# Depthwise convolution of the conv module: six channel tiles on TensorE and two on VectorE in place of five and three

## The chip, the cores and the metric

The kernel runs on one core of one Trainium2 chip. The time is the device time of one execution in microseconds (us). A profile of one execution records every instruction of the five engines: TensorE (PE, with its weight loads as PEld), VectorE (DVE), ScalarE (ACT), GpSimd (POOL) and SyncE (SP), which here only issues DMAs.

## The reference

The program computes one inference step of a two-layer decoder, for 512 prompt tokens and 8 x 8 sample tokens (576 columns in all), model width 1024, in float32. The first layer has a Conformer convolution module between two feed-forward blocks, the second has dilated attention between two more. The part that matters here is that module:

```
def conformer_conv(h, prev, w_pw1, b_pw1, w_dw, b_dw, ln_g, ln_b, w_pw2, b_pw2):
    a, g = jnp.split(h @ w_pw1 + b_pw1, 2, axis=-1)
    u = a * jax.nn.sigmoid(g)
    u_ext = jnp.concatenate([prev.astype(u.dtype), u], axis=1)
    c = lax.conv_general_dilated(u_ext, w_dw[:, None, :].astype(u.dtype), window_strides=(1,),
                                 padding='VALID', dimension_numbers=('NWC', 'WIO', 'NWC'),
                                 feature_group_count=CONV_INNER) + b_dw
    c = jax.nn.silu(layernorm(c, ln_g, ln_b))
    return c @ w_pw2 + b_pw2, u_ext[:, -(CONV_WIDTH - 1):]
```

The depthwise convolution gives every one of the 1024 channels its own 31 taps over time. The LayerNorm behind it needs the mean over all channels, so it can't begin before the last channel tile is convolved.

## The kernel before

Activations lie with channels on the 128 partitions, in KD = 8 channel tiles, and tokens along the free axis. The order of the work is written out by hand for each engine; engines wait for one another through semaphores, and each engine and each DMA queue works its list in order.

**The stage.** The pointwise projection pw1 is 16 chunks c of 128 output channels, two for each channel tile ct (the value half and the gate half). For each chunk ACT and then DVE split the float32 weights into a high and a low part (L995, L1488), PE runs 48 matmuls (L2101), DVE scales the result out of PSUM (L1844), and after the second chunk of a tile ACT applies the sigmoid (L1261) and DVE writes `u` for that tile into `ucat` (L1855, L1856) and raises `u_ready`. The weight buffers and PSUM banks let PE be some two chunks ahead of DVE: chunk c waits for its own split and for the scaled-out result of chunk c-2.

**Two ways to convolve.** The constant CD is how many of the eight tiles go to DVE, and CP = KD - CD is how many go to PE.
- On DVE (function `taps`), a tile is 31 taps, each a pair of instructions, one over the 512 prompt columns (L1828) and one over the 64 sample columns (L1829). In the tiles behind the first one ACT does the first tap (L1255, L1257). DVE does a few taps whenever the list has room: 4 after each even chunk, and `taps(3 if ct <= CD else 12)` after each tile, for tiles 1 to 6; what is left follows behind the chunk loop.
- On PE (function `convolve`), a tile is 32 matmuls of 512 columns and 32 of 64 columns (L2401, L2407), each with 32 output channels and the taps as its weights `dW`. These weights are made by POOL (L901). The input `uV` is four shifted copies of the tile's `ucat`, made by DMAs, eight of them on SP's queue (function `spread`, L677) and eight on POOL's (L936), into one of two buffers. ACT brings the result from PSUM to `cT` (`conv_out`, L1243, L1244).

**Places.** The first tile for PE is tile CD. Its convolve stands behind chunk 2*CD + 4, the following ones behind each odd chunk from 2*CD + 5 on, and the last behind the chunk loop. Behind each convolve but the first of the loop stands `mean_of` (L2421), which adds one finished tile into the sum for the LayerNorm's mean; the others stand behind the loop. On SP the uV loads of tile ct stand behind the weight load of chunk 2*ct + 7. On ACT `conv_out(ct - 1 - CD)` stands behind the sigmoid of tile ct.

**The end of the stage.** PE: the last chunk, a convolve, a `mean_of`, transposes of the new state (L2456, L2458), more `mean_of`, the last convolve, bias tables (L2467, L2468), `mean_of(7)`, one more bias table (L2473, which waits for ACT's cast of the table E2, L1289), and `mean_of(CD - 1)`. Then DVE subtracts the mean (L1867), ACT squares (L1302), PE sums (L2496) and pw2 follows. ACT casts E2 only behind the last `conv_out`. SP loads the tables E, after waiting for `uv_in0` to show three uV loads, behind its last `spread`.

Of the kernel before, what the change touches and what calls it, by code (L numbers as in the profile page):

```python
# [18 lines left out]
HALF = TOK // 2  # L19
KD, KF = D // P, FF // P  # L20
CW = 31
CD = 3
CP = KD - CD
NQ, NS = 4, 8
HEADS, HD, AW = 8, 64, 512
# [262 lines left out]
def trunk_program(nc, I, O):  # L288
# [286 lines left out]
    def _(sp):  # L575
# [91 lines left out]
        def spread(ct):  # L667

            n = ct - CD
            sp.wait_ge(S["u_ready"], ct + 1)  # L670
# [15 lines left out]

        done = CD
        for c in range(4, 24):
# [170 lines left out]
    def _(pool):  # L859
# [37 lines left out]
        def taps(n):  # L897

            if n >= 2:
                pool.wait_ge(S["conv_mm"], n - 1)  # L900
            nc.gpsimd.tensor_tensor(  # L901
                dW[:, n % 2], id32[:].rearrange("p (a b c) -> p a b c", a=1, b=1).broadcast_to([P, 4, NS, 32]),
                wQ[:, :, CD + n, :].rearrange("p a (b c) -> p a b c", c=1).broadcast_to([P, 4, NS, 32]),
                ALU.mult).then_inc(S["taps_ready"], 1)
# [23 lines left out]
        for n in range(CP):  # L928
            taps(n)

            pool.wait_ge(S["u_ready"], CD + n + 1)
            if n == 0:
                pool.wait_ge(S["st_ready"], KD)
            for g in range(2, 4):
                for q in range(NQ):
                    pool.dma_start(uV[32 * q:32 * q + 32, n % 2, g, :],  # L936
                                   ucat[32 * g:32 * g + 32, CD + n, q:q + VW]).then_inc(S[f"uv_gp{n % 2}"], 16)

# [1905 lines left out]
```

## Time and profile before

| what | us |
|---|---|
| median of 3 runs | 2265.07 |
| lowest and highest run | 2263.11, 2266.39 |
| time of the profiled execution | 2262.11 |
| its span, first to last instruction | 2260.2 |
| pw1 chunks 3 to 15 with the convolutions, on PE | 440.85 to 571.9 |
| LayerNorm and its surroundings, until pw2's first matmul on PE | 571.9 to 592.3 |

Starts in the rows below are counted from the span's start. A row of PE stands for a run of matmuls of one line; those of the convolution and of the mean, in plain float32, count as two each, those of pw1 as one. PEclk is the clock that TensorE was granted, 1.00 being its upper level of 2.4 GHz and 0.50 its lower of 1.2 GHz.

### The profile page before, as it was taken

What the parts mean: (1) busy time and instruction counts of PE and PEld (TensorE: products, weight loads), DVE (VectorE), ACT (ScalarE), POOL (GpSimd) and SP (SyncE); (2) the same over time, 40 slices, a digit from 0 to 9 for tenths busy, and PEclk for the clock granted to TensorE, in tenths of its full rate; (3) what the DMA queues carried; (4) which work ended last, traced back from release to release, by engine and by line L of the source; (5) the groups of instructions that cost most, each with busy time, mean ns of one, the idle gap of its engine ahead of it and who ended that gap; (6) DMA issues with size and microseconds to landing.
All of it is one profiled execution on the core that took longest, in us unless ns stands there. A gap on an engine that the chain in (4) does not pass through costs nothing.

```text
span 2260.2 us, 41620 instructions
## 1 busy us (share of the span) xinstructions
PE 2214.9 (98%) x17636; PEld 2102.0 (93%) x17636; DVE 1617.6 (72%) x2138; ACT 890.1 (39%) x1167; POOL 137.3 (6%) x191
## 2 busy tenths in 40 slices
PE   7999999999999999999999999999999999999998
PEld 6999999987799999998889999999987789999998
DVE  7983995699789849953358956984445479947963
ACT  6431443222654314432234422442145555413442
POOL 0000000323010000001001000001001100000001
PEclk8999999999899999999999999999999999999999
DMA  5543443554244435423439533532959933233321
GB/s 156 158 151 110 151 156 93 164 141 126 72 147 150 140 100 164 153 83 90 132 107 304 173 114 99 168 115 73 240 148 281 253 113 94 75 98 96 88 77 55
DMA packets 372091, 305.61 MB, mean 135 GB/s; under 512 B 13798, under 2 KB 338414, under 8 KB 371050
## 3 DMA queue, kind: packets, MB, share of 16 engines
q1 hardware_dynamic: 365485, 232.06, 36.4%
q0 software_dynamic: 6464, 71.76, 9.2%
q8 instruction: 86, 1.41, 0.3%
q14 instruction: 44, 0.35, 0.1%
q10 hardware_dynamic: 12, 0.02, 0.0%
HBM read 284.45 MB, written 70.54 MB: 157 GB/s over the span
## 4 chain that ended last, share of the span: by engine, by line
PE 88%; DVE 6%; issue 2%; ACT 2%; DMA 2%; SPq 1%; DVEq 0%; ACTq 0%
PE ps L2101 34%; PE ps L2157 13%; PE ps L2159 13%; PE ps L2158 13%; PE ps L2565 2%; PE ps L2563 2%; PE ps L2564 2%; PE ps L2401 2%; PE ps L2609 1%; DMA kc<-in_cache_kv_w 1%; DVE blk L1572 1%; PE ps L2725 1%; DVE hlS L1549 1%; PE ps L2663 1%; PE ps L2716 1%
## 5 line engine op out<-in xcount | busy, mean ns | idle before, releaser
L1087 ACT CAST hlS<-blk 128x1024 fp32r<-128x1024 f32 x176 | 184.3, 1053 | 207.0 <-PE ps L2159 169.4
L2101 PE MATMUL ps<-actH,oWA 128*128 128x288 f32 x1408 | 250.4, 296 | 0.0
L2101 PE MATMUL ps<-actH,oWB 128*128 128x288 f32 x1408 | 250.0, 296 | 0.0
L1716 DVE SCALAR_TENSOR_TENSOR cs<-ps,rstd 128x576 f32<-128x576 f32 x64 | 48.5, 757 | 246.9 <-PE ps L2101 246.9
L1549 DVE TENSOR_TENSOR hlS<-blk,hlS 128x1024 fp32r<-128x1024 f32 x176 | 213.5, 1216 | 2.4 <-ACT hlS L1087 2.4
L2157 PE MATMUL ps<-tM,hlA 128*128 128x288 f32 x704 | 212.4, 302 | 2.9 <-DVE hlA L1549 2.4
L2157 PE MATMUL ps<-tE,hlS 128*128 128x288 f32 x704 | 208.5, 296 | 4.1 <-DVE hlS L1549 4.1
L2101 PEld LDWEIGHTS ps<-actH,oWA 128*128 128x128 f32 x1408 | 209.0, 189 | 1.2 <-DVE cs L1611 0.6
L2101 PEld LDWEIGHTS ps<-actH,oWB 128*128 128x128 f32 x1408 | 209.0, 189 | 0.0
L2157 PE MATMUL ps<-tM,hlS 128*128 128x288 f32 x704 | 208.2, 296 | 0.0
L2158 PE MATMUL ps<-tM,hlA 128*128 128x288 f32 x704 | 208.0, 295 | 0.0
L2159 PE MATMUL ps<-tM,hlA 128*128 128x288 f32 x704 | 207.5, 295 | 0.0
L2158 PE MATMUL ps<-tE,hlS 128*128 128x288 f32 x704 | 207.5, 295 | 0.0
L2159 PE MATMUL ps<-tE,hlS 128*128 128x288 f32 x704 | 207.2, 294 | 0.0
L2158 PE MATMUL ps<-tM,hlS 128*128 128x288 f32 x704 | 207.2, 294 | 0.0
L2159 PE MATMUL ps<-tM,hlS 128*128 128x288 f32 x704 | 206.9, 294 | 0.0
L1488 DVE TENSOR_TENSOR wHL<-wst,wHL 128x1024 fp32r<-128x1024 f32 x64 | 82.2, 1285 | 116.8 <-ACT wHL L995 116.7
L1116 ACT ACTIVATE ta<-ta 128x576 f32<-128x576 f32 x88 | 60.5, 687 | 266.5 <-DVE ta L1631 266.5
L2101 PE MATMUL ps<-hH,wHL 128*128 128x288 f32 x896 | 158.5, 297 | 0.0
L1549 DVE TENSOR_TENSOR hlA<-blk,hlA 128x1536 fp32r<-128x1536 f32 (+2 forms) x104 | 156.0, 1504 | 0.9 <-ACT hlA L1087 0.9
L1087 ACT CAST hlA<-blk 128x1536 fp32r<-128x1536 f32 (+2 forms) x104 | 132.3, 1280 | 47.6 <-PE ps L2101 29.7
L2101 PE MATMUL ps<-actL,oWA 128*128 128x288 f32 x704 | 150.8, 296 | 0.0
(323 smaller groups left out, 5363.3 us busy)
## 6 DMA issues: line engine op xcount, KB each, us to landing
blk<-in_ffn_w_in SPq DMA_DIRECT2D x352, 256.0 KB, 4.1
raws<-in_ffn_w_out SPq DMA_DIRECT2D x64, 704.0 KB, 4.7
out_kv_sample<-in_cache_kv_w POOLq DMA_DIRECT2D x8, 4064.0 KB, 16.8
out_kv_sample<-in_cache_kv_w POOLq DMA_DIRECT2D x8, 2016.0 KB, 9.2
wst<-in_conv_w_pw SPq DMA_DIRECT2D x24, 512.0 KB, 4.1
wst<-in_w_kv SPq DMA_DIRECT2D x24, 512.0 KB, 3.8
kc<-in_cache_kv_w SPq DMA_DIRECT2D x40, 256.0 KB, 9.1
kc<-in_cache_kv_w SPq DMA_DIRECT2D x8, 1024.0 KB, 7.7
```

The costliest lines, as they stand in the source:

```text
L1087: nc.scalar.copy(o, a).then_inc(S["f_h"], 1)
L1116: nc.scalar.activation(ta[:], ta[:], ACT.Silu).then_inc(S["silu_done"], 1)
L1488: nc.vector.tensor_tensor(wL[:, s % 2, 0:size], wst[:, s, 0:size], wH[:, s % 2, 0:size].bitcast(f32), ALU.subtract).then_inc(S["w_ready"], 1)
L1549: nc.vector.tensor_tensor(o, a, h.bitcast(f32), ALU.subtract).then_inc(S["f_ready"], 1)
L1716: nc.vector.scalar_tensor_tensor(px[m % 2], pair(2 + m % 2), 0.5, rstd[:], ALU.mult, ALU.mult).then_inc(S["px_ready"], 1)
L2101: nx = nc.tensor.matmul(outs[t], a, b[:, t, :], start=start and first, stop=stop and b is xh and not first)
L2157: nc.tensor.matmul(out, wh[:, cols], TERM[what][:, p, 0], start=p == 0, stop=False)
L2158: nc.tensor.matmul(out, wh[:, cols], TERM[what][:, p, 1], start=False, stop=False)
L2159: nx = nc.tensor.matmul(out, wl[:, cols], TERM[what][:, p, 0], start=False, stop=p == KD // 2 - 1)
L2401: nc.tensor.matmul(ps[32 * g:32 * g + 32, 0, :], dW[:, s, g, k, :], uV[:, s, g, 4 * k:4 * k + SEQ], start=k == 0, stop=k == NS - 1, tile_p ...
L2563: nc.tensor.matmul(ps[:, t, :], xh, a, start=k == 0, stop=False)
L2564: nc.tensor.matmul(ps[:, t, :], xh, b, start=False, stop=False)
```

## The change

One constant is changed. Everything in the stage that depends on it moves with it.

```
@@ -19,7 +19,7 @@
 HALF = TOK // 2
 KD, KF = D // P, FF // P
 CW = 31
-CD = 3
+CD = 2
 CP = KD - CD
 NQ, NS = 4, 8
 HEADS, HD, AW = 8, 64, 512
```

Tile 2 goes from DVE to PE, so there are six convolves. On PE the first of them stood behind chunk 10, with nothing of the kind ahead of it, and one followed behind chunk 11:

```order
L2101 MATMUL ps<-hH,wHL 128x288 x2
L2401 MATMUL ps<-uV,dW 32x512 x32
L2407 MATMUL ps<-uV,dW 32x64 x32
L2101 MATMUL ps<-hH,wHL 128x288 x2
L2101 MATMUL ps<-hL,wHL 128x288 x2
```

Now there is one behind chunk 8 and, after another chunk, this one behind chunk 9, with a `mean_of`; those behind chunks 11, 13, 15 and behind the loop stand where they did:

```order
L2101 MATMUL ps<-hH,wHL 128x288 x2
L2401 MATMUL ps<-uV,dW 32x512 x32
L2407 MATMUL ps<-uV,dW 32x64 x32
L2421 MATMUL ps<-cT,ones 128x288 x2
L2101 MATMUL ps<-hH,wHL 128x288 x2
L2101 MATMUL ps<-hL,wHL 128x288 x2
```

What moved is one convolve, with its `mean_of`, into the chunk loop: the one behind chunk 10 is gone, and those behind chunks 8 and 9 are new. Behind the loop PE's list loses one `mean_of`, ahead of the last convolve:

```order
 L2456 MATMUL ps<-ident,ucat 30x128 x8
 L2458 MATMUL ps<-ident,un 64x128 x8
-L2421 MATMUL ps<-cT,ones 128x288 x6
+L2421 MATMUL ps<-cT,ones 128x288 x4
 L2401 MATMUL ps<-uV,dW 32x512 x32
 L2407 MATMUL ps<-uV,dW 32x64 x32
```

On DVE the 30 pairs of taps of tile 2 are gone, and since `taps(3 if ct <= CD else 12)` gives 12 from tile 3 on, nine taps of the remaining tiles come earlier: behind the `u` of tile 3, ahead of the weight split of chunk 10. At the end of the loop DVE's list now reads, from the last split of pw1 to the LayerNorm, with no tap in it:

```order
L1488 TENSOR_TENSOR wHL<-wst,wHL 128x1024
L1844 TENSOR_TENSOR tb<-ps,rstd 128x576
L1855 SCALAR_TENSOR_TENSOR ucat<-ta,par,tb 128x512
L1856 SCALAR_TENSOR_TENSOR ucat<-ta,par,tb 128x8x8
L1844 TENSOR_TENSOR ta<-ps,rstd 128x576
L1844 TENSOR_TENSOR tb<-ps,rstd 128x576
L1855 SCALAR_TENSOR_TENSOR ucat<-ta,par,tb 128x512
L1856 SCALAR_TENSOR_TENSOR ucat<-ta,par,tb 128x8x8
L1488 TENSOR_TENSOR wHL<-wst,wHL 128x1024
L1867 SCALAR_TENSOR_TENSOR cT<-ps,cT 128x576 x8
```

What moved there is the work that stood between these rows: 24 pairs of taps came after the last L1856 before, and none does now.

On SP and POOL there is one more uV load of eight DMAs each, and POOL makes the weights of one more tile. SP's row of uV loads for the first PE tile stands one pair of weight loads earlier (behind chunk 11's load, not chunk 13's). On ACT the first tap of tile 2 goes, and `conv_out` of the first PE tile comes in, both in the list of tile 3. The waits for `uv_in0` are counted as before (three loads), and the load of the sixth PE tile goes to the other buffer, so SP's loads of the tables E no longer wait for the last uV load to land.

## Rows read from the trace of the kernel before

**Rows 1.** The page's first part: each engine's busy time in the span.

```profile
PE 2214.9 (98%) x17636; PEld 2102.0 (93%) x17636; DVE 1617.6 (72%) x2138; ACT 890.1 (39%) x1167; POOL 137.3 (6%) x191
```

**Rows 2.** The chain that ended last, in time order: start us, us, what.

```profile
440.85 51.20 PE ps L2101 x384
...
514.42 1.17 PE ps L2421 x4
...
550.22 7.00 PE ps L2401 x64
...
561.03 2.91 PE ps L2421 x12
563.94 7.00 PE ps L2401 x64
570.95 0.94 PE ps L2407 x64
```

**Rows 3.** Busy time by stretch: us, engines (instructions), PEclk, DMA share, GB/s.

```profile
485.00:575.00 90.00, 89.60 (x984) 61.28 (x983) 84.11 (x155) 20.89 (x29) 26.12 (x44) 1.00 0.50 137
575.00:600.00 25.00, 22.22 (x146) 16.41 (x147) 19.64 (x29) 21.00 (x31) 0.00 (x0) 0.73 0.15 43
```

**Rows 4.** DVE in time order near the LayerNorm: start, us, instruction, [idle before].

```profile
574.42 0.75 DVE L1828 SCALAR_TENSOR_TENSOR cT<-ucat,par,cT 128x512 f32<-128x512 f32 x1
...
575.40 0.75 DVE L1828 SCALAR_TENSOR_TENSOR cT<-ucat,par,cT 128x512 f32<-128x512 f32 x1
576.07 0.28 DVE L1829 SCALAR_TENSOR_TENSOR cT<-ucat,par,cT 128x64 f32<-128x64 f32 x1
...
577.71 5.41 DVE L1867 SCALAR_TENSOR_TENSOR cT<-ps,cT 128x576 f32<-128x576 f32 x8 [0.23 <-PE ps L2421]
```

**Rows 5.** PE in time order, the same stretch.

```profile
574.89 1.19 PE L2473 MATMUL ps<-E2r,sel 128*128 128x512 f32 x4 [0.40 <-ACT E2r L1289]
...
576.44 1.24 PE L2421 MATMUL ps<-cT,ones 128*128 128x288 f32 x4
```

**Rows 6.** ACT in time order, the same stretch.

```profile
572.49 0.31 ACT L1244 ACTIVATE cT<-ps,par 128x64 f32<-128x64 f32 x1
572.69 2.15 ACT L1289 CAST E2r<-E 128x2352 fp32r<-128x2352 f32 x1
...
578.75 0.67 ACT L1302 ACTIVATE ta<-cT 128x576 f32<-128x576 f32 x1
```

**Rows 7.** Everything on tile cT, the taps' line: duration ns min/median/max, first and last start.

```profile
L1828 DVE SCALAR_TENSOR_TENSOR cT<-ucat,par,cT x90: 740/752/2456, 445.2 to 575.4; 128x512 f32<-128x512 f32 x90
```

**Rows 8.** DVE in time order inside the pointwise stage: ends of tiles 2, 3 and 7.

```profile
465.33 0.28 DVE L1856 SCALAR_TENSOR_TENSOR ucat<-ta,par,tb 128x64 f32<-128x64 f32 x1
...
477.45 0.28 DVE L1856 SCALAR_TENSOR_TENSOR ucat<-ta,par,tb 128x64 f32<-128x64 f32 x1
...
480.48 1.22 DVE L1488 TENSOR_TENSOR wHL<-wst,wHL 128x1024 fp32r<-128x1024 f32 x1
...
552.59 0.28 DVE L1856 SCALAR_TENSOR_TENSOR ucat<-ta,par,tb 128x64 f32<-128x64 f32 x1
```

**Rows 9.** SyncE's queue in time order: start, us that the issuing took.

```profile
477.76 5.67 SPq L677 DMA_DIRECT2D uV<-ucat  x8
...
536.43 22.64 SPq L677 DMA_DIRECT2D uV<-ucat  x16
563.37 0.33 SPq L702 DMA_DIRECT2D E<-in_onehot  x1
```

**Rows 10.** Everything on tile uV: the loads, and their time from issue to landing.

```profile
DMA to landing us min/median/max: 2.4/3.9/5.7
```

**Rows 11.** Busy time and granted clock by stretches of 2 us behind the convolution.

```profile
578.00:580.00 2.00, 0.45 (x8) 0.16 (x8) 2.00 (x4) 1.99 (x4) 0.00 (x0) 1.00 0.56 158
...
582.00:584.00 2.00, 1.42 (x24) 0.48 (x24) 2.00 (x3) 1.68 (x4) 0.00 (x0) 0.50 0.00 0
...
592.00:594.00 2.00, 2.00 (x9) 1.97 (x9) 1.95 (x4) 1.92 (x4) 0.00 (x0) 0.50 0.00 0
```

More of the change, by code:

```diff
@@ L21 @@
 CW = 31
-CD = 3
+CD = 2
 CP = KD - CD
```

## The prediction

> **What bounds the kernel now.** I read the page's first part, then the chain of work that ended last, then the busy time by stretch, and then each engine's list around the two ends of the convolution. The first part puts PE at 98% of the span and DVE at 72% [rows 1], but that is an average; the change touches only the pw1 stage, so that stage has to be read by itself. The chain says who holds its end: from 440.85 us, where chunk 3 begins, to 571.89, where the fifth convolve ends, it never leaves PE [rows 2]. The stretch from 485 to 575 shows PE busy for 89.60 of 90 us at the full granted clock, and DVE for 84.11 [rows 3]. So both engines are full there, and the change takes work from one to give it to the other. What counts is which of them the next step, the LayerNorm, waits for. DVE's last tap ends at 576.35 [rows 4], 4.5 us behind PE's last convolve, and looks like the late one. But PE's list shows that the last `mean_of`, which adds that tile, starts at 576.44, right behind a bias table product that began at 574.89 because it waited for ACT's cast of E2 [rows 5], and that cast runs from 572.69 to 574.84, directly behind the `conv_out` that PE's last convolve releases [rows 6]. So DVE's taps and the path PE convolve, ACT `conv_out`, ACT E2, PE table come to the same point within 0.1 us. The second path hangs on PE. I take PE as the bound of the stage and of its end.
>
> **What is taken away.** Tile 2's 30 pairs of taps: the trace has 90 of them for three tiles [rows 7], and two neighbours start 0.98 us apart [rows 4], so DVE loses 29.4 us of work. Its last tap moves from behind the loop to tile 5. On the path this is worth at most what DVE is late by now: `mean_of` could start some 0.1 us sooner. I count 0; the ends are 0 and, if the E2 product were not in front of it, 3.6 us: from the end of `conv_out` at 572.80 [rows 6] a `mean_of(7)` and a last `mean_of` of about 1 us each could have been done by 574.8, against a first mean subtraction at 577.71 now with its PE work ended just before [rows 4, 5]; less the semaphores, somewhat under 3 us. I take 0 because the E2 product stays in front.
>
> **What is added on PE.** One convolve is 7.00 us for the 512-column matmuls and 0.94 for the 64-column ones [rows 2]; I take 7.9 us. One `mean_of` moves from the run of three behind the loop, where each is 2.91 / 3 = 0.97 us, to behind a convolve, where it takes 1.17 us [rows 2]: +0.2 us. Nothing hides this, since PE has no gap in the stage: 8.1 us.
>
> **Does PE have to wait for anything new?** Chunks are 51.20 / 8 = 6.40 us [rows 2], so chunk 8 ends at 479.25 and the first convolve begins there. Its input, `u` of tile 2, is ready at 465.61 [rows 8]. SP's eight DMAs take 5.67 us to issue [rows 9], and the slowest uV load took 5.7 us to land [rows 10]: 477.0, 2.3 us early. POOL's half is issued from the same moment beside it. The convolve ends at 487.2, chunk 9 at 493.6. The second convolve's input is ready at 477.73 [rows 8] and landed by 489.1, 4.5 us early. It and its `mean_of` end at 502.6, where chunk 10 begins. DVE has nine more taps ahead of that chunk's weight split, 8.8 us: the split starts at about 489.3 in place of 480.48 [rows 8] and is done by 490.5, 12 us early. Later tiles give DVE 16 taps each as before, while PE's pace per tile is two chunks and a convolve, as long as DVE's list; DVE doesn't fall further behind, and from tile 6 on it has no tap. ACT stands in `conv_out` until the first convolve ends at 487.2 and splits chunk 10 then, in time for DVE. The weight loads behind SP's earlier uV loads shift by up to 8.8 us and are still read a chunk or two later. Each of these costs 0.
>
> The last convolve is the tight place. Now `u` of tile 7 is written at 552.87 [rows 8], and SP, which has issued the last uV load by 536.43 + 22.64 = 559.07, goes on to the tables E at 563.37 [rows 9], when that load has landed; that is 13.15 us behind the end of chunk 15 at 550.22. PE reaches the convolve at 563.94, 13.72 us behind it [rows 2]. The slack is 0.57 us. With one `mean_of` less in between, PE is there 12.75 us behind the chunk, and waits for 0.4 us. The bounds are 0 (if the load lands as much sooner) and 1.4 us more (a landing of 5.7 us [rows 10] in place of some 4.3).
>
> **The end of the stage** keeps its order: `conv_out`, E2, table product, last `mean_of`, mean subtraction, squares from 578.75 on [rows 6]. ACT sets it, and moves with the last convolve. Its price doesn't change, except for the clock: over 575 to 600 us PE was granted 0.73 [rows 3], which at two levels of 1.00 and 0.50 is 13.5 us at the lower one. It fell behind a stretch in which PE was busy for 0.45 of 2 us, and pw2 began at 0.50 [rows 11]. That pause stays. Where the falls lie against the work may differ: 5 us more or less of PE work at the lower level would be 2.5 us either way. I take 0. Everything behind is released by PE's progress and moves along.
>
> **The sum** is 7.9 + 0.2 + 0.4 + 0 = +8.5 us. Against its own time the profiled execution would go from 2262.11 to 2270.6 us. That execution is 3.0 us below the median of the runs, 2265.07, and 1.0 below the fastest of them; the median would go to 2273.6 us, +0.38%. A measurement of this kernel can tell about 0.2% from no change, 4.5 us: below 2260.5 is faster, above 2269.6 slower.
>
> **Rivals.**
> - *The sixth input is late.* SP sends the tables E, 1.4 MB, right behind its last uV load and no longer waits for that to land. If they share the DMA engines so that the landing takes twice its 4.3 us, the last convolve waits 4.3 us more: +12.8, 2277.9 us. Against it: the uV load is ahead in the same queue. 7%.
> - *PE has room* (not slower). PE is counted busy for 89.60 of 90 us, but its weight loads only for 61.28 [rows 3], which leaves 28.7 us, three and a half convolves. If matmuls can close up, the added one goes into that room, and only the 0.4 us wait is left: 2265.5 us. This decides if the chunks around a convolve are longer than those far from one. They aren't: from 515.59 to 550.22 the chain holds chunks 12 to 15, a convolve and a `mean_of`; (34.63 - 9.06) / 4 = 6.39 us, the 6.40 of the chunks with no convolve near [rows 2]. 4%. The Trainium skill, Perfetto Trace Analysis, section "Identifying the Most-Contended Engine", has it that matmul busy time is a poor measure of how close PE is to its limit, and that weight loads' busy share is a better one. By that rule this rival would be the forecast; no row here bears it out.
> - *The clock is kept.* If all 13.5 us at the lower level ran at the upper one and PE set the pace throughout, that gives back 6.7 us: +1.8, 2266.9 us, no change. It decides if the pause behind the last `mean_of` goes, and nothing in the change shortens it. 5%.
> - *DVE was the late one.* Then the under 3 us above come back: +5.6, 2270.7 us. It decides if PE waits for the last tap and not for E2. 3%.
> - *Faster.* To gain 4.5 us the change would have to win back 13 us; I find no place for it. 2%.
>
> **How the numbers follow.** The forecast has 79%, and its own range is 2270 to 2277: the sum with its bounds (7.9 to 9.9), the clock's 2.5 us either way, hardly both at their ends, and the runs' 1.5 us around their median. The range for 8 in 10 reaches some way to the late input and to the late DVE: 2269 to 2278. Slower holds the forecast, the late input and the late DVE, 79 + 7 + 3 = 89%, less 1 for a forecast that comes out small: 88%. Same holds the room, the clock and that 1: 10%. Faster 2%.
>
> **What the profile after would show.** In the chain, six runs of 7.00 and 0.9 us in place of five, the first at about 479.3, with chunks still at 6.40 us and PE unbroken to about 580.3. A gap of about 0.4 us ahead of the last convolve. DVE's last tap near 531, and DVE free from the `u` of tile 7 to the mean subtraction; that first subtraction at about 586.2, and pw2's first matmul 8.5 us behind its 592.3. I am wrong if PE waits ahead of chunks 10 to 13 (DVE or ACT too late), if convolves overlap chunks, or if the time from the last convolve to pw2 shrinks by over a microsecond.

## The result, and the profile after

| | before | after |
|---|---|---|
| median of 7 runs each, us | 2265.05 | 2273.71 |
| lowest and highest | 2263.11, 2266.77 | 2271.16, 2275.37 |
| profiled execution, and its span | 2262.11, 2260.2 | 2273.71, 2271.8 |

The change makes the kernel slower: ratio 1.0039, 95% interval 1.003 to 1.0049, or +8.7 us. The forecast was 2273.6 us and slower, by one extra convolve on an engine with no gap to put it in. The interval of the measured change is 6.8 to 11.1 us.

The first part of the page of after, the span and each engine's busy time, has for [rows 1]:

```profile
span 2271.8 us, 41835 instructions
...
PE 2227.2 (98%) x17764; PEld 2108.8 (93%) x17764; DVE 1590.3 (70%) x2078; ACT 891.0 (39%) x1167; POOL 144.1 (6%) x200
```

PE's share is the same 98% of a longer span; DVE gave up 27 us of busy time and PE took 12. Eight of these are the convolve, the others in part matmuls at the lower clock, below. What DVE gave up bought nothing. The chain of work that ended last, in time order (start us, us, what), answers [rows 2]:

```profile
479.51 7.00 PE ps L2401 x64
486.52 0.89 PE ps L2407 x64
487.41 6.58 PE ps L2101 x48
493.99 7.00 PE ps L2401 x64
500.99 0.89 PE ps L2407 x64
501.88 1.17 PE ps L2421 x4
503.05 12.78 PE ps L2101 x96
...
559.52 7.00 PE ps L2401 x64
...
570.33 1.94 PE ps L2421 x8
572.27 0.84 issue
573.11 7.07 PE ps L2401 x64
580.18 0.93 PE ps L2407 x64
```

The reader should see the added convolve at 479.51, the next one behind a single chunk, chunks still at 6.4 us each (12.78 for two), and one gap, 0.84 us of "issue", ahead of the last convolve. Up to that gap PE is never without work. The engines' lists in time order around the LayerNorm, one after the other for PE, DVE and ACT (start, us, instruction, [idle before]), answer [rows 4 to 6]:

```profile
584.12 1.19 PE L2473 MATMUL ps<-E2r,sel 128*128 128x512 f32 x4 [0.39 <-ACT E2r L1289]
...
585.67 1.24 PE L2421 MATMUL ps<-cT,ones 128*128 128x288 f32 x4
```

```profile
563.81 1.22 DVE L1488 TENSOR_TENSOR wHL<-wst,wHL 128x1024 fp32r<-128x1024 f32 x1 [1.64 <-ACT wHL L995]
586.95 5.41 DVE L1867 SCALAR_TENSOR_TENSOR cT<-ps,cT 128x576 f32<-128x576 f32 x8 [21.91 <-PE ps L2421]
```

```profile
581.72 0.31 ACT L1244 ACTIVATE cT<-ps,par 128x64 f32<-128x64 f32 x1
581.92 2.15 ACT L1289 CAST E2r<-E 128x2352 fp32r<-128x2352 f32 x1
...
587.99 0.67 ACT L1302 ACTIVATE ta<-cT 128x576 f32<-128x576 f32 x1
```

DVE now stands idle for 21.91 us ahead of the mean subtraction, which starts as late behind the last convolve as before. PE still waits for the cast of E2, with 0.39 us as in [rows 5].

For the rest, each profiled execution was measured on PE's own list, from the start of chunk 3 (440.62 us before, 440.88 after) to the end of the last convolve, and from there on. All columns are in us, worked out from starts and durations of rows such as those above:

| kernel | chunk 3 to end of last convolve | gap ahead of it | then to mean subtraction | to squares | to pw2's first matmul | to the feed-forward |
|---|---|---|---|---|---|---|
| before | 131.22 | none | 5.87 | 6.91 | 20.46 | 74.09 |
| after | 140.19 | 0.84 | 5.88 | 6.92 | 23.03 | 76.02 |
| a1 | 131.22 | none | 5.89 | 6.91 | 20.43 | 73.98 |
| a2 | 131.23 | none | 5.84 | 6.63 | 23.05 | 75.77 |
| a3 | 131.23 | none | 5.50 | 6.29 | 18.37 | 72.34 |
| a4 | 138.98 | none | 5.88 | 6.91 | 23.21 | 75.83 |
| b1 | 139.63 | 0.27 | 5.86 | 6.90 | 23.04 | 76.00 |
| b2 | 140.26 | none | 4.24 | 5.03 | 18.79 | 72.48 |
| c1 | 131.23 | none | 5.87 | 6.91 | 18.90 | 72.34 |
| c2 | 139.96 | 0.60 | 5.88 | 6.91 | 18.90 | 72.25 |
| c3 | 131.23 | none | 5.84 | 6.63 | 18.79 | 72.88 |

The kernels are those of the experiments. The difference of the two spans, 11.6 us, is 0.26 before chunk 3, 8.97 to the end of the last convolve, 1.93 from there to the feed-forward, and 0.4 in all the rest.

### The profile page after: what moved, and what is told of

Read it like the earlier page. It is cut to its first block, busy times and chain, and to the rows that moved or that the text cites. A ratio compares the mean times of both kernels' runs of the same rounds, so it can differ in the third digit from the quotient of the medians.

```text
span 2271.8 us, 41835 instructions
## 1 busy us (share of the span) xinstructions
PE 2227.2 (98%) x17764; PEld 2108.8 (93%) x17764; DVE 1590.3 (70%) x2078; ACT 891.0 (39%) x1167; POOL 144.1 (6%) x200
## 4 chain that ended last, share of the span: by engine, by line
PE 88%; DVE 6%; issue 2%; ACT 2%; DMA 1%; SPq 1%; DVEq 0%; ACTq 0%
PE ps L2101 34%; PE ps L2157 13%; PE ps L2159 13%; PE ps L2158 13%; PE ps L2565 2%; PE ps L2563 2%; PE ps L2564 2%; PE ps L2401 2%; DMA kc<-in_cache_kv_w 1%; PE ps L2609 1%; DVE blk L1572 1%; DVE hlS L1549 1%; DVE hlA L1549 1%; PE ps L2716 1%; PE ps L2725 1%
## 5 line engine op out<-in xcount | busy, mean ns | idle before, releaser
L1087 ACT CAST hlS<-blk 128x1024 fp32r<-128x1024 f32 x176 | 184.5, 1054 | 205.7 <-PE ps L2159 169.0
```

Source lines behind the costliest of these rows:

```text
L1087: nc.scalar.copy(o, a).then_inc(S["f_h"], 1)
```

## Experiments

The lines of the diffs are cut to what is changed. Times are compared with runs of the kernel before on the same chip.

### The relief without the price: a1, a2, a3

Here the question is what DVE's relief is worth by itself. Kernel a1 leaves out 29 of the 30 taps that DVE does for tile 2 and changes nothing on PE:

```
-                if k == 0 and ct:
+                if k == 0 and ct or ct == 2 and k < CW - 1:
                     continue
-                if k == 1 and ct:
+                if ct and k == (CW - 1 if ct == 2 else 1):
                     dve.wait_ge(S["tap_first"], ct)
```

> The kernel before (three tiles on DVE) with 29 of tile 2's 31 taps left out on DVE, so its output for those 128 channels is not the convolution; PE's and ACT's lists are unchanged. It is the relief of DVE without the price on PE. If PE and ACT's cast of E2 set the end of the stage (theory PE), the time is that of before, within 0.3 us in the trace: the mean subtraction still starts 5.8 us behind the end of the last convolve, the squares 6.9 us behind it. If DVE's taps are the late ones (theory DVE), the mean subtraction starts up to 3 us sooner and the time falls by as much.

Measured: 2263.45 us against 2264.42, ratio 0.9994 (0.9985 to 1.0003): no change that can be told. DVE's list in time order:

```profile
575.89 5.41 DVE L1867 SCALAR_TENSOR_TENSOR cT<-ps,cT 128x576 f32<-128x576 f32 x8 [21.99 <-PE ps L2421]
```

This execution came to chunk 3 1.8 us sooner than that of before, so the starts themselves say nothing; counted from the end of the last convolve, the mean subtraction is at 5.89 us, where it was at 5.87. DVE waits 21.99 us for it. Taking 29 of a tile's 31 taps off VectorE is worth nothing.

The chain of work of the kernel before, behind its last convolve, shows one reason more than the prediction gives. It goes over to ACT with `conv_out` and doesn't leave ACT until the squares:

```profile
575.92 1.28 ACT L1106
...
577.42 1.43 ACT Rsb L1297 x3
578.84 0.57 ACT ta L1302
```

After the cast of E2 come the cast of Ebad, the loading of the square root's table (L1106) and the bias rows (L1297), and they end at 578.84, when DVE's first tile (577.71 plus 5.41 / 8) has been ready for 0.4 us. So ACT's own list is a path of its own to the squares, beside the two that the prediction compares, and an earlier `mean_of` alone couldn't have brought the squares forward.

Kernel a2 takes the other path away, with all taps in place:

```
-        conv_out(CP - 1)
         act.wait_ge(S["bias_in"], 16 * 2)
         nc.scalar.copy(E2r[:].rearrange("p a b -> p (a b)"), E2[:].rearrange("p a b -> p (a b)")).then_inc(S["bias_h"], 1)
         nc.scalar.copy(Ebadr[:], Ebad[:]).then_inc(S["bias_h"], 1)
+        conv_out(CP - 1)
         root_table()
...
-        mean_of(KD - 1)
         pe.wait_ge(S["bias_h"], 5)
         pe.wait_ge(S["sel_ready"], 1)
         sample_bias(ps[:, 7, :], C1, C2, 1)
+        mean_of(KD - 1)
```

> The kernel before, with ACT's casts of the tables E2 and Ebad ahead of the last conv_out in place of behind it, and the table product ahead of mean_of(7) on PE. Theory PE: the cast path was 0.1 us ahead of DVE's last tap, so taking the path away alone brings DVE's taps to the front: the mean subtraction stays within 0.3 us of 577.7 and the squares move by 0.4 us at most. Theory that the casts alone set the end: up to 2 us sooner.

Measured: 2263.62 us, ratio 0.9995 (0.9986 to 1.0004), and squares 0.28 us sooner behind the last convolve (6.63 for 6.91). The chain of work of a2 shows why not more. In before it ran through ACT's list here; now it runs through DVE's taps:

```profile
575.19 0.75 DVE cT L1828
...
576.20 1.25 PE ps L2421 x4
577.47 2.76 DVE cT L1867 x4
```

The paths do end together: with DVE's gone ACT's holds the stage, and with ACT's shortened DVE's holds it, within 0.3 us. Kernel a3 has both edits, so its diff is both of those above.

> Both of the preceding edits together (29 taps of tile 2 left out, casts first). Theory of two paths that end together: neither edit alone moves the squares by more than 0.4 us, both together bring them forward by 2.1 us (mean subtraction at about 575.8, squares at 576.7 in place of 578.75, then held by ACT's table load and bias rows). If either path alone were the bound, this kernel would be as fast as the one of a1 or a2 that removed it.

Measured: 2263.88 us, ratio 0.9995 (0.9986 to 1.0004), squares at 6.29 us. The direction is right and the size isn't: 0.6 us in place of 2.1. The chain begins with something that I hadn't looked at, the landing of the tables:

```profile
564.48 7.06 DMA Ebad<-in_unseen_sample
571.56 2.16 ACT E2r L1288
```

The tables E land at 571.56 only, 0.8 us before the last convolve ends, so casting them first makes `conv_out` late (it starts at 574.69). In the kernel before, DVE's relief and this reordering give 0.6 us together. Whether the relief would be worth more with the tables there sooner wasn't tried on this kernel: SP loads them only when PE is done with chunk 15. In b2 below they are there 3.5 us ahead of the end of the last convolve, and it is 1.9 us.

### The price without the relief: a4

```
-            for k in range(NS):
-                for g in range(4):
-                    nc.tensor.matmul(ps[32 * g:32 * g + 32, 0, :], dW[:, s, g, k, :], uV[:, s, g, 4 * k:4 * k + SEQ],
+            for _ in range(2 if n == 1 else 1):
+                for k in range(NS):
+                    for g in range(4):
+                        nc.tensor.matmul(ps[32 * g:32 * g + 32, 0, :], dW[:, s, g, k, :], uV[:, s, g, 4 * k:4 * k + SEQ],
...
```

> The kernel before, with the 64 matmuls of its second convolve issued twice (the same result is written again). It is the price on PE without the relief of DVE. Theory PE: every chunk keeps its 6.40 us, the last convolve ends 7.9 us later, the whole takes 7.9 us more, 2273.0 us. Rival 'PE has room': below 2 us more. Against the changed kernel it lacks the moved mean_of (0.2 us) and the gap ahead of the last convolve, so it should be some 0.2 to 1.1 us faster than that.

Measured: 2272.14 us against 2264.42, +7.7 us, ratio 1.0032 (1.0021 to 1.0043). The chain of work around the doubled convolve:

```profile
506.94 7.00 PE ps L2402 x64
513.94 0.89 PE ps L2408 x64
514.84 6.87 PE ps L2402 x64
521.70 0.89 PE ps L2408 x64
522.60 1.17 PE ps L2422 x4
```

(L2402 and L2408 are L2401 and L2407 of before, moved by a line.) The second round takes 6.87 + 0.89 = 7.76 us, and the end of the last convolve is 138.98 - 131.22 = 7.76 us later: all of it is on the path. This settles the rival that PE has room because its weight loads are busy for only two thirds of the stretch [rows 3]. By the rule of the Trainium skill that the prediction weighed (Perfetto Trace Analysis, "Identifying the Most-Contended Engine") there was a third of slack; here an added 7.76 us of matmuls came through whole. And a4, which keeps all of DVE's taps, is within 1.6 us of the changed kernel, which is rid of a third of them.

### The gap ahead of the last convolve: b1

The changed kernel, with one line more ahead of SP's loads of the tables E:

```
         sp.wait_ge(S["uv_in0"], 16 * 8 * 3)
+        sp.wait_ge(S["uv_in1"], 16 * 8 * 3)
```

> The changed kernel, but SP waits for all uV loads of both buffers before it loads the tables E, as it in effect did before. In the changed kernel PE idles 0.84 us ahead of the last convolve, where I had forecast 0.4. Theory A: the surplus of 0.44 us is the tables' loads running beside the last uV load; then the gap falls to about 0.4 us. Theory B: the landing of the uV load varies by that much by itself; then the gap stays anywhere from 0.2 to 0.9 us. In the time neither shows.

SP's queue in time order (start, us of issuing), first of after and then of b1, and PE's row at the gap in b1:

```profile
544.21 24.00 SPq L677 DMA_DIRECT2D uV<-ucat  x16
568.31 0.48 SPq L702 DMA_DIRECT2D E<-in_onehot  x1
```

```profile
572.24 0.33 SPq L703 DMA_DIRECT2D E<-in_onehot  x1
```

```profile
572.25 7.07 PE L2402 MATMUL ps<-uV,dW 128*32 128x512 f32 x64 [0.27 <-issue]
```

In after the tables go out at 568.31, at once behind the last uV load; in b1 they wait until 572.24, when it has landed. PE starts the convolve at 572.25, so it is this landing that ends the gap. The gap is 0.27 us in b1, 0.84 in after and 0.60 in c2, which sends the tables as after does. In before the load landed 13.15 us behind chunk 15, which made the forecast of 0.4. The rows point to theory A, that the tables' loads run beside the uV load and delay it by some 0.3 to 0.6 us, but there is one execution of b1, and I can't put an interval on it. In the time nothing shows, as expected: 2273.30 us, 1.0038 of before (1.0024 to 1.0052).

### Using DVE's early end: b2

If DVE is done 40 us early, the order behind it can be made to profit. This is the changed kernel with `mean_of(1)` ahead of the last convolve, where PE had its gap, and ACT's casts and table load ahead of the last `conv_out`:

```
-        for k in range(CD - 1):
+        for k in range(CD):
             mean_of(k)
         convolve(CP - 1)
...
-        conv_out(CP - 1)
         act.wait_ge(S["bias_in"], 16 * 2)
...
         root_table()
+        conv_out(CP - 1)
...
-        mean_of(KD - 1)
...
         sample_bias(ps[:, 7, :], C1, C2, 1)
-        mean_of(CD - 1)
+        mean_of(KD - 1)
```

> The changed kernel, using DVE's early end: mean_of(1) goes ahead of the last convolve (its taps are done by 539), and ACT's casts of E2 and Ebad and the loading of the square root's table go ahead of the last conv_out, where ACT stood idle for 5.7 us. mean_of(1) fills the idle time of PE there. Theory PE: the end of the last convolve moves back by at most 0.4 us (the extra mean_of is longer than the gap), the squares come some 3.5 to 4.5 us sooner behind it, the time falls to about 2270 us, which is still 4 to 5 us above the kernel before. If it falls below 2265 the convolve's price was not on the path.

Measured: 2270.82 us against 2264.26, ratio 1.0033 (1.0020 to 1.0045), where after had 1.0039 (1.003 to 1.0049): some 2 us less, not clear of the intervals. In the trace the steps are there. PE's gap is filled (no idle time ahead of the last convolve, whose end is at 140.26 and 140.19 us), and the squares come 5.03 us behind it in place of 6.92. That is 1.9 us, not the 3.5 to 4.5 expected. The chain of work of b2 behind the last convolve has the reason:

```profile
580.45 0.34 PE ps L2467
...
581.94 1.12 PE ps L2473 x4
...
583.48 1.18 PE ps L2421 x4
...
584.69 2.10 DVE cT L1867 x3
```

It stays on PE. The bias table products (L2467 to L2477) stand between the last convolve and the last `mean_of` and take 3.0 us without a gap. ACT casts the tables from 576.92, when they have landed, and comes to `conv_out` at 581.57, 1.1 us after PE is done, but that ends at 582.44, a microsecond before PE's list gets to the `mean_of` that needs it. ACT then waits 1.62 us for DVE ahead of the squares. So the bound is PE's list again; moving the products wasn't tried. Even with the relief put to use, six tiles on PE stay slower than five.

### The clock: c1, c2, c3

Between the last `mean_of` and the squares' sums PE has a pause, and its clock falls behind it [rows 11]. In c1 (from before) and c2 (from after) 11 small matmuls go into the pauses; c3 is c1 with the edit of a2.

```
         for k in range(KD):
+            for _ in range(8 if k == 0 else 1 * (k % 2 == 0)):
+                nc.tensor.matmul(ps[:, 1, 0:P], ident[:], ones[:], start=True, stop=True)
             pe.wait_ge(S["csq_ready"], k + 1)
```

> The kernel before, with 11 small matmuls (ident times ones into a bank that is overwritten later) in PE's pauses around the squares: 8 ahead of the first wait, 3 ahead of later ones. Theory: PE's clock falls to its lower level because of the pause behind the last mean_of; with the pause filled the granted clock stays at 1.00 from 575 to 600 us (0.73 before), and the time falls by 2 to 4 us, to about 2262 us, with less scatter from run to run. Rival: the fall has another cause and the time stays at 2265 or rises by up to 1 us for the added matmuls.

> The changed kernel with the same 11 matmuls in the pauses. If the clock's fall adds the same to both kernels and only scatters, c2 minus c1 is 8.1 + the gap ahead of the last convolve (0.4 to 0.9) = 8.5 to 9.0 us, with a narrower interval than the 8.7 us between the two kernels as they are. If part of the change's price is the clock, c2 minus c1 is smaller, 6 to 7 us.

> The kernel before with the two small gains that showed in traces but not clearly in times, together: ACT's casts of E2 and Ebad ahead of the last conv_out (squares 0.3 us sooner), and PE's pauses around the squares filled with 11 small matmuls (feed-forward 1.8 us sooner behind the last convolve). If the clock's fall costs time, the feed-forward starts 72.0 us behind the last convolve in place of 74.1 and the time falls by 1 to 2 us against before, to 2263 us. If what is saved there is lost again later (the theory that c1's unchanged median suggests), the time stays within 0.7 us.

Measured: c1 2264.04 us against 2264.26, ratio 1.0003 (0.9994 to 1.0012); c2 2271.90, ratio 1.0034 (1.0022 to 1.0046); c3 2264.91 against 2264.72, ratio 1.0002 (0.9993 to 1.0011). Busy time by stretches of 10 us (as [rows 3]: the third number from the end is the granted clock) of c1 and then of c2:

```profile
580.00:590.00 10.00, 9.59 (x98) 6.37 (x94) 6.88 (x10) 7.76 (x13) 0.00 (x0) 1.00 0.28 82
590.00:600.00 10.00, 9.15 (x55) 8.68 (x55) 9.28 (x13) 9.73 (x14) 0.00 (x0) 0.83 0.00 0
```

```profile
590.00:600.00 10.00, 9.22 (x86) 6.47 (x80) 6.90 (x9) 7.78 (x12) 0.00 (x0) 0.95 0.20 55
600.00:610.00 10.00, 9.59 (x62) 9.26 (x62) 8.62 (x13) 9.09 (x13) 0.00 (x0) 0.88 0.00 0
```

With the pause filled the clock holds at 1.00 behind the squares; it still falls once later, about where pw2 begins. In the stage c1 is 1.75 us ahead of the kernel before (72.34 for 74.09 to the feed-forward) and c2 3.8 us ahead of the changed one (72.25 for 76.02). That the filling does this is not quite shown: a3 has nothing in its pause and is as quick, at 72.34. Its clock (as [rows 11]) held too, behind a pause with PE as idle as in before:

```profile
578.00:580.00 2.00, 0.45 (x8) 0.16 (x8) 2.00 (x4) 1.85 (x5) 0.00 (x0) 1.00 0.00 0
580.00:582.00 2.00, 1.36 (x24) 0.47 (x24) 2.00 (x4) 2.00 (x4) 0.00 (x0) 1.00 0.00 0
```

Of the eight profiled executions of the table without the filling, seven have the fall around the squares; of the three with it, none has. With the clock the same in both, the two kernels reach the feed-forward 8.64 us apart: (139.96 + 72.25) - (131.23 + 72.34). That is the cleanest figure for the change, and the clock is no part of it; the expectation for c2 minus c1 was 8.5 to 9.0. The medians give 7.9, with intervals of 2 to 3 us to either side of each.

The gain of c1 in the stage is not found in its time, and my expectation of 2 to 4 us failed. In the profiled executions, from the feed-forward to the end, before took 1614.3 us, after 1614.7, a4 1612.4, c1 1616.7, c3 1617.2 and c2 1615.3. The other kernels with five or six convolves lie between 1613.0 and 1615.8. The part behind the stage scatters by more than the gain, and the filled ones are at its upper end. The rows of DVE say where: from the scaling of a query tile in the second layer (L1938, 1009 us after the feed-forward begins) to a later L1542 the kernel before takes 181.9 us, the others without the filling 179.6 to 182.4, and c1, c3 and c2 184.3, 184.5 and 182.5. Up to that stretch c1 keeps its lead to within 0.1 us, and behind it c1 runs as before to 0.1 us again. So the gain is not lost at once behind the stage. Whether the filled kernels lose their gain there, 1000 us later, or three executions came out so, stays open.

### The other way: b3

```
-CD = 3
+CD = 4
...
-        sp.wait_ge(S["uv_in0"], 16 * 8 * 3)
+        sp.wait_ge(S["uv_in0"], 16 * 8 * 2)
```

The second edit follows from the first: with four tiles on PE the first buffer gets two loads.

> The constant moved the other way: four channel tiles on DVE, four on PE (SP's wait ahead of the tables E counts two loads in uv_in0, since there are no more). PE loses 8.1 us of work, DVE gains 30 pairs of taps, 29.4 us. With three tiles the two end within 0.1 us of each other, so here DVE is the late one by itself: the last mean_of starts on the last tap, and the mean subtraction comes about 29 us later than before, the squares 0.8 us behind it. The time rises by 28 to 30 us, to about 2293 us. If PE still set the end it would fall by 8 us to 2256 us; if the work were shared out evenly between them it would rise by about 10.

Measured: 2292.49 us against 2264.72, +27.8 us, ratio 1.0121 (1.0105 to 1.0136). PE's list and then DVE's at the end of the stage:

```profile
575.42 2.29 PE L2421 MATMUL ps<-cT,ones 128*128 128x288 f32 x4 [20.21 <-DVE cT L1829]
577.63 8.82 PE L2401 MATMUL ps<-uV,dW 128*32 128x512 f32 x64
...
604.79 2.29 PE L2421 MATMUL ps<-cT,ones 128*128 128x288 f32 x4 [12.75 <-DVE cT L1829]
```

```profile
607.12 5.41 DVE L1867 SCALAR_TENSOR_TENSOR cT<-ps,cT 128x576 f32<-128x576 f32 x8 [1.25 <-PE ps L2421]
```

The mean subtraction comes at 607.12 in place of 577.71, 29.4 us later (29.1 counted from chunk 3), which is about 30 pairs of taps at 0.98 us. PE idles 20.21 us ahead of its last convolve, because a `mean_of` in front of it in the queue waits for DVE's third tile, and 12.75 us ahead of the last `mean_of`. So three tiles are the crossing: from there one tile more on DVE costs 28 us, one more on PE 8.7.

## Why the prediction was right

**The bound.** PE was taken as the bound of the stage and, through ACT's cast of E2, of its end, with DVE's last tap 0.1 us beside it. a1 and a4 show each half by itself: DVE's relief changes nothing, PE's load comes through whole. What joins the last convolve to the squares is not only the way through the E2 product on PE that the prediction follows, but ACT's own list behind it, which hangs on PE just the same; that is why the conclusion held.

**What is taken away**, 0 us with 3 us as the far end: a1 measured 0.02 us in the trace. The far end was too far. (Its first figure, 3.6 us, is a slip too: 577.71 less 574.8 is 2.9.) a3 shows that with the E2 product out of the way 0.6 us is there; the prediction looked neither at ACT's list up to the squares nor at the landing of the tables.

**What is added**, 7.9 + 0.2: from chunk 3 to the end of the last convolve after takes 8.97 us more, 0.84 of it the gap, so 8.13 us of work.

**The wait**, 0.4 us: the mechanism was right (one `mean_of` less, a load that lands at the same distance from chunk 15), the size was half of what came, 0.84. That the sum still came out within 0.1 us of the median is luck: its parts by the trace make 8.97 us, and the medians can tell the change only to 2 us either way. The first rival, tables' loads beside the uV load, was to double the landing time and cost 4.3 us; it is in b1 as some tenths.

**No new waits in the loop**: right, but the margins weren't what I worked out. The weight split of chunk 10 was forecast for 489.3 us and came at 492.85, and DVE's last tap for near 531 and came at 538.4. DVE's list in time order and POOL's, in after, show what was missing:

```profile
528.08 2.77 DVE L1829 SCALAR_TENSOR_TENSOR cT<-ucat,par,cT 128x64 f32<-128x64 f32 x1
530.88 0.75 DVE L1828 SCALAR_TENSOR_TENSOR cT<-ucat,par,cT 128x512 f32<-128x512 f32 x1
```

```profile
528.83 1.93 POOL L901 TENSOR_TENSOR dW<-id,wQ 128x1024 f32<-128x1024 f32 x1
```

A tap of 0.28 us takes 2.77 while POOL multiplies the next tile's weights. I had priced DVE's list at 0.98 us for each pair throughout, and the maximum of 2456 ns in [rows 7] should have said otherwise. It cost nothing, since PE had some 9 us in hand.

**The end of the stage**, 0 us but for 2.5 us of clock either way: mean subtraction and squares moved by 0.01 us against the last convolve, in after as in a4. The clock is the largest part, 1.93 us, of why the profiled execution grew by 11.6 us and not 8.5. At the end of the stage (stretches of 2 us, granted clock third from the end, as [rows 11]) it falls behind the pause and is still down at 602, where before had come back to 1.00 from 588 to 590:

```profile
588.00:590.00 2.00, 0.91 (x16) 0.32 (x16) 2.00 (x4) 1.94 (x5) 0.00 (x0) 1.00 0.00 0
...
592.00:594.00 2.00, 1.78 (x28) 0.58 (x24) 1.49 (x2) 1.32 (x2) 0.00 (x0) 0.50 0.00 0
...
600.00:602.00 2.00, 2.00 (x8) 1.82 (x9) 1.02 (x3) 1.87 (x3) 0.00 (x0) 0.50 0.00 0
```

pw2 begins 23.03 us behind the last convolve, where it began at 20.46. a2, which has five convolves, has 23.05, so this isn't the change's doing; the medians, +8.7 us, don't show it.

## What to carry to other kernels

When two engines look full, work out which of them the next stage waits for before moving work from one to the other: the gain is only what the late path is late by, here 0.1 us, and the price is the whole of the added work if the other engine's chain has no gap. Two runs settle it without building the new version: leave the work out on one engine, and do it twice on the other. Where the trace shows two paths that end together, look for a third behind them (here ACT's own list, and behind it the landing of a table) before counting what freeing both would give.

## What the runs showed of the hardware

A GpSimd multiply draws out a VectorE operation with two inputs that runs beside it. In before and after one operation stretched beside each multiply of the stage, but for the last of after, when VectorE was idle: a tap of 0.28 us took 1.94 to 2.77, one of 0.75 took 2.35 to 2.46, a weight split of 1.22 took 2.60. The short taps ended 0.1 us behind the multiply. The multiply itself took 1.93 us with VectorE idle too, and 2.38 in one case beside it. The Trainium skill has this in GPSIMD Engine Reference, section "Specifications": GpSimd's SBUF interfaces are shared with VectorE, with contention for VectorE instructions with two SBUF inputs. These taps have two, and the trace agrees.

The fall of the clock is not the same from one execution to the next. Behind a pause in which PE was busy for 0.45 of 2 us it fell from 2.4 to 1.2 GHz in before and stayed up in a3; where it fell, it was down for one stretch or for a longer one with nearly the same work, and the time from the last convolve to pw2 went from 18.4 to 23.2 us. In the three executions with matmuls of 128 columns in the pause it stayed up.
